# Last norm before the gate: transposing the plain stream and applying the row factor in the sigmoid

## The reference, cut to what matters

```python
def rmsnorm_2(x, w):
    xf = x.astype(jnp.float32)
    y = xf * lax.rsqrt(jnp.mean(xf * xf, axis=-1, keepdims=True) + EPS)
    return (y * w.astype(jnp.float32)).astype(x.dtype)

h = h + (jax.nn.silu(gate) * up) @ w_down[i]
ple_gate = jax.nn.sigmoid(rmsnorm_2(h, ple_norm_w[i]) @ w_ple_gate[i])
h = h + ple_gate * (p[i] @ w_ple_proj[i])
return rmsnorm_2(h, final_norm_w)
```

## Time and profile before

| | |
|---|---|
| median of the runs | 819.86 us (817.09 to 819.89) |
| span of the profiled execution | 815.9 us |
| PE busy | 780.6 us, 96% of the span |
| PEld / DVE / ACT / POOL busy | 669.7 / 540.0 / 414.7 / 92.5 us |
| granted PE clock, mean | 0.993 of full |

### The profile page before, as it was taken

One profiled execution on the slowest core, in us unless ns is written; L12 is line 12 of the kernel. 1 busy time (PEld: TensorE's weight loads), 2 busy tenths in 40 slices (PEclk: granted clock), 3 DMA queues, 4 the chain that ended last, 5 costly groups with the idle time before them and its releaser, 6 DMA issues. The chain is left out here.

```text
span 815.9 us, 11773 instructions
## 1 busy us (share of the span) xinstructions
PE 780.6 (96%) x4599; PEld 669.7 (82%) x4599; DVE 540.0 (66%) x714; ACT 414.7 (51%) x582; POOL 92.5 (11%) x150
## 2 busy tenths in 40 slices
PE   4899999999999999999989999999999999999996
PEld 3777787777789898988789998988888998988884
DVE  0673789977588778887478786654466666654465
ACT  2623413453676776644266555556364545543264
POOL 4000130401100000000060313210100000000000
PEclk9999999999999999999999999999999999999998
DMA  9963667732456556669536342321465655545611
GB/s 309 361 242 119 217 241 254 277 131 91 129 189 199 168 191 206 206 219 322 182 82 206 104 156 54 105 102 52 153 205 185 206 170 190 192 155 194 226 59 51
DMA packets 107900, 144.83 MB, mean 178 GB/s; under 512 B 6343, under 2 KB 70352, under 8 KB 107856
## 3 DMA queue, kind: packets, MB, share of 16 engines
q1 hardware_dynamic: 100512, 137.38, 50.7%
q10 hardware_dynamic: 7280, 6.83, 2.7%
q0 software_dynamic: 64, 0.01, 0.0%
HBM read 142.10 MB, written 2.10 MB: 177 GB/s over the span
## 5 line engine op out<-in xcount | busy, mean ns | idle before, releaser
L2074 PE MATMUL ps<-h_parts,w_hi 128*128 128x512 f32 x504 | 179.6, 396 | 0.0
L1276 DVE TENSOR_TENSOR w_lo<-raw,w_hi 128x2048 fp32r<-128x2048 f32 (+1 forms) x61 | 135.6, 2230 | 63.9 <-ACT w_hi L666 63.7
L666 ACT CAST w_hi<-raw 128x2048 fp32r<-128x2048 f32 (+1 forms) x61 | 112.9, 1852 | 78.2 <-PE ps L1950 56.6
L2073 PE MATMUL ps<-h_parts,w_lo 128*128 128x256 f32 x504 | 140.5, 279 | 0.0
L1284 DVE TENSOR_TENSOR w_lo<-raw,w_hi 128x2048 fp32r<-128x2048 f32 x44 | 100.7, 2289 | 16.2 <-ACT w_hi L674 15.7
L2074 PEld LDWEIGHTS ps<-h_parts,w_hi 128*128 128x128 f32 x504 | 94.6, 188 | 19.5
L2073 PEld LDWEIGHTS ps<-h_parts,w_lo 128*128 128x128 f32 x504 | 95.0, 188 | 3.3
L674 ACT CAST w_hi<-raw 128x2048 fp32r<-128x2048 f32 x44 | 84.0, 1908 | 0.0
L1948 PE MATMUL ps<-w_hi,act_hi 128*128 128x512 f32 x176 | 69.0, 392 | 0.0
L1950 PE MATMUL ps<-w_hi,act_lo 128*128 128x512 f32 x176 | 68.5, 389 | 0.0
L1949 PE MATMUL ps<-w_lo,act_hi 128*128 128x512 f32 x176 | 68.5, 389 | 0.0
(11 more groups left out here) (419 smaller groups left out, 1557.4 us busy)
## 6 DMA issues: line engine op xcount, KB each, us to landing
raw<-in_ffn_up_w SPq DMA_DIRECT2D x22, 1024.0 KB, 5.0
raw<-in_w_gate_up SPq DMA_DIRECT2D x22, 1024.0 KB, 5.0
raw<-in_ada_w SPq DMA_DIRECT2D x16, 1024.0 KB, 5.2
raw<-in_w_in SPq DMA_DIRECT2D x14, 1024.0 KB, 5.2
raw<-in_m_in_w SPq DMA_DIRECT2D x11, 1024.0 KB, 5.2
raw<-in_ffn_down_w SPq DMA_DIRECT2D x10, 1024.0 KB, 5.3
raw<-in_w_down SPq DMA_DIRECT2D x10, 1024.0 KB, 5.0
raw<-in_m_out_w SPq DMA_DIRECT2D x4, 1024.0 KB, 5.0
```

Of the source, the lines that this page charges most:

```text
L666: act.copy(part_view(w_hi, s), raw_view(split[s])).then_inc(hi_ready, 1)
L1276: dve.tensor_tensor(part_view(w_lo, s), raw_view(split[s]), part_view(w_hi, s).bitcast(F32), ALU.subtract).then_inc(lo_ready, 1)
L2073: pe.matmul(both[:, 0], lo[:, k, w], h_hi[:, k, :], start=False, stop=False)
L2074: ins = pe.matmul(both, hi[:, k, w], h_parts[:, :, k, :], start=False, stop=k == KD - 1)
```

## The change

Blocks of the plain stream are transposed with the identity (`flip`, the helper at L2114 that the kernel uses for its other transposes); `diagonal` is dropped for this norm, and its wait with it. `tile_turned` waits for the stream's halves instead (`x_upd`). The feature factor is still applied in `tile_hi` and `tile_lo`. The row factor becomes the `scale` operand of the sigmoid that reads the product out of PSUM, a column with one number per token; the sigmoid of tile t waits for that tile's factor. On ACT `tile_hi(0)` now stands ahead of the third sum of squares and of the cast of the second group.

```diff
             for t in range(TT):
                 norm_half("norm5", 12, t, t, 0)
+            tile_hi(0)
             norm_half("norm5", 12, 2, 0, 1)
             hi_until(at["ple_g"][0] + 2)
-            tile_hi(0)
             norm_half("norm5", 12, 3, 1, 1)
...
-                    bank_out(sig[:, i % 2, :], i, "sig_ready", ACT.Sigmoid)
+                    if n == 0:
+                        act.wait_ge(S("rstd"), base("rstd", "norm5") + t + 1)
+                    r_ = SS["norm5"] + t
+                    act.activation(sig[:, i % 2, :], ps[:, i, :], ACT.Sigmoid, scale=rstd[:, r_:r_ + 1]).then_inc(S("sig_ready"), 1)
...
             residual(1, 0)
-            diagonal("norm5", 0, base("rstd", "norm5") + 1)
             lo_until(at["ple_g"][0] + 2)
...
             tile_lo(0)
-            diagonal("norm5", 1, base("rstd", "norm5") + 2)
...
-                pe.wait_ge(S("diag"), base("diag", "norm5") + t + 1)
                 for k in range(KD):
-                    ins = pe.matmul(tile_bank(t, k), x[:, t, k * P:(k + 1) * P], diag[:, t, :], start=True, stop=True)
+                    if k % 4 == 0:
+                        pe.wait_ge(S("x_upd"), 12 + TT * (k // 4) + t + 1)
+                    ins = flip(tile_bank(t, k), x[:, t, k * P:(k + 1) * P])
                     if k % 4 == 3:
                         ins.then_inc(S("tr"), 1)
```

More of the change, by code:

```diff
@@ L160, in two_blocks @@
             "t0_done": (("mix_out", 1), ("down", 1), ("att_out", 1), ("down2", 1), ("ple_g", 1)),
-            "diag": (("norm1", 4), ("norm2", 2), ("norm3", 2), ("norm4", 2), ("norm5", 2)),
+            "diag": (("norm1", 4), ("norm2", 2), ("norm3", 2), ("norm4", 2)),
         }
```

## The result

The changed kernel takes 822.33 us against 819.12, ratio 1.0057 with a 95% interval of 1.0037 to 1.0077: about half a per cent slower. Between the medians lie 3.2 us, where 3.9 was forecast. Timed a second time, beside another set of runs of the kernel before, it is 821.75 against 817.55, ratio 1.0052 [1.0034, 1.0070], 4.2 us between the medians.

A forecast was written before the change was run, and what follows sets the result against it. PE was taken as the bound, with almost no gap from 780 to 808 us. Terms: 2.9 + 0.15 - 0.91 + 0.1 + 0.1 = 2.3, plus 1.6 for the clock, 3.9 on 819.86: 823.8 us, range 819.8 to 826.4.

The forecast's parts named there:

- Transposes and the wait ahead of them: PE, tile 0: no wait for the diagonal and eight transposes in 0.79 us, so the next matmul starts 1.54 earlier.
- The bound that had transposes as slow as matmuls: PE: with transposes as slow as the old matmuls, only 0.3 us gained on the first tile, nothing on the second.
- The cast and the list behind it: ACT's second-group cast starts 3.2 us later, behind `tile_hi(0)`; DVE's list passes it on whole, `tile_lo(0)` at about 788.7.
- The pause: PE stands still 4.4 us before tile 0's low-part matmuls, waiting for DVE; these start 2.9 late.
- The second tile: PE, tile 1: transposes give back 0.91 us, less 0.1 because `tile_hi(1)` starts a little later against PE.
- The clock: PE's granted clock falls to 0.50 in the pause, making the matmuls behind it slow; cost 1.6 us.
- the clock holds: Rival: same pause on PE but no slow matmuls, 2.3 us later in all, 822.2; chance 0.22.
- the slow clock lasts: Rival: PE's clock falls early in the pause and stays low through tile 1, 5.5 us later, 825.4; chance 0.13.
- The sigmoid's scale: Last sigmoid in the tail: its scale column costs between 0 and 0.1 us, taken as 0.1.
- no change: Measured outcome for the whole kernel within about 0.5% (4.1 us), taken as what a measurement can tell; chance 0.58.
- slower: Measured outcome for the whole kernel more than about 4.1 us slower; chance 0.39.
- The rival on the other side: ACT passes its new order in time, so PE has no pause: 2.35 us gained, 817.5; chance 0.07.

The follow-up runs named there:

- e1: The changed kernel with ACT's old order: third sum of squares and second group's cast ahead of `tile_hi(0)` again; 817.03 us against 817.68, ratio 0.9986.
- e2: The kernel before with only `tile_hi(0)` moved ahead of the second group's cast on ACT; 824.04 us against 817.68, ratio 1.0058.
- e5: e1 plus, on PE, both groups' high products of tile 0, then tile 1's transposes, ahead of the low products; 815.96 us against 817.68, ratio 0.9973.
- e4: e5 without the early transposes of tile 1, which stand behind tile 0's low products again; 815.71 us in one run, against 817.55.
- e3: The changed kernel with 18 extra matmuls, their result unused, filling PE's pause on tile 0; 820.92 us against 817.68, ratio 1.0029.
- e6: e5 with ordinary float32 matmuls against the identity in place of its transposes; 816.95 us against 817.55, ratio 0.9995.

## Why the prediction was right, point by point

- **Transposes and the wait ahead of them.** 1.54 earlier for the first tile was forecast; from the landmark to the six matmuls it is 1.03 (779.22 to 780.25) against 2.56: 1.53. The bound that had transposes as slow as matmuls did not come true.
- **The cast and the list behind it.** A cast 3.2 later was forecast; against the landmark it is 3.26. `tile_lo(0)` starts 8.50 behind the landmark (787.72 - 779.22) against 5.24 before (785.49 - 780.25): 3.26 again, passed on whole, as e1 and e2 then showed from both sides.
- **The pause.** 4.4 forecast, 4.40 in the row. The low parts start 8.89 behind the landmark and before 5.84 (786.09 - 780.25), so they are 3.05 late where 2.9 was told.
- **The second tile.** This term was mis-sized. 0.91 back with 0.1 for a wait was forecast, but from the transposes' start to the next matmul it is 1.15 (793.54 to 794.69) where the transposes need 0.79: 0.36 of wait for ACT's first block, so 0.55 came back against the 1.70 of before. e5, which has no such wait, is 0.39 shorter than e4, which has it.
- **The clock.** 1.6 forecast. The four low-part matmuls take 1.37 (788.11 to 789.48) against 0.94 before (786.09 to 787.03): 0.43, of which 0.15 is DVE's pace. The eight behind them take 3.15 (789.48 to 792.63) and not 1.85 as in e3 (792.44 to 794.29): 1.30. Together 0.28 + 1.30 = 1.6, and e3 gets 1.6 back. The size was right, the moment was not: the prediction had the clock fall in the pause, and it fell 0.8 us behind the pause's end. All of the slow stretch came under matmuls, as at 84 us, from which the 1.6 was taken; by the prediction's own reckoning a fall early in the pause would have cost less. That the row at 84 us was a good measure is in part luck, since the clock had been at 0.50 from 78 to 80 us too, ahead of the pause of 2.06. The rivals "the clock holds" and "the slow clock lasts" did not happen in the two profiles of this kernel.
- **The sigmoid's scale.** 0.69 in the tail against 0.60: 0.09, as bounded.
- **The sum.** On the profiled execution: stretch +4.25, tail +0.08 (819.2 - 810.90 against 815.9 - 807.68), and the landmark 1.03 earlier by what other stages did, which makes the 3.3 between the spans. By the mechanism the change costs 4.3, where 2.3 + 1.6 = 3.9 was told; the difference is the second tile's wait (0.26) and the low parts (0.15). The ratios, 0.57 and 0.52% of 819, are 4.7 and 4.3 us.
- **The time and the chances.** That 822.33 lies near the 823.8 told is in part luck. The base was the median of three runs, 819.86; the larger sets of the kernel before have 817.68 and 817.55, so the base was some 2 us high and the cost 0.4 low. A run's time is 1.7 to 1.9 us above its own span in every run on record, so the profile of 815.9 was of a run of about 817.7 and not of the median one. The ends of the range do not follow from what is said of them: the cases of 822.2 and 825.4 with half of 2.8 give 820.8 and 826.8, not 819.8 and 826.4; the measured time lies in both. And "no change" had 0.58 because 4.1 us was taken for the least that a measurement can tell: both intervals, some 0.2% to either side, lie clear of 1, so "slower", at 0.39, was given too little.
- **The rival on the other side** (ACT in time, 2.35 faster) needed the cast early; e1 gives it that, and the stretch is 0.55 shorter than before, not 2.35, since the low parts still bind by 0.76 and tile 1 waits. Only with PE's list rearranged, in e5, is it 1.88.

## What to carry to other kernels

Before an instruction is moved up on an engine that works down a list, look at what the engine waits for at the new place and at what then stands behind it: here 2 us of blocks and 0.8 us of a sum of squares went ahead of a cast that could have started 0.4 us before them (0.50 behind the landmark against 0.94), and the delay ran through a second engine's list to the bound engine. A pause on PE can have a second price behind it, in the clock; count the slow matmuls, and if a pause can't be avoided, other products that are ready may stand in it, as the second group's high products do in e5. To judge changes of a few microseconds, measure between two landmarks in the trace, since the medians carry the luck of the other stages.

## What the runs showed of the hardware that was not expected

The clock did not fall in the pauses of this place but behind them. It was at 1.00 through 4.40 us without a matmul (two profiles) and through 3.21 (e2), and fell each time 0.5 to 0.8 us after PE had begun again.

The same pause can be followed by a slow clock in one profile and not in another. Ahead of the transposes of an earlier norm PE waits about 2.36 us in every profile of this study; before, the window behind it had 1.00, in the changed kernel, whose program is the same there, it is

```profile
416.00:420.00 4.00, 4.00 (x24) 4.00 (x24) 2.74 (x7) 3.61 (x9) 3.45 (x9) 0.60 0.11 6
```

Four of the nine profiles have the fall there (both of the changed kernel, e5 and e6), five have not; what decides it stays open. From the end of that wait to the matmuls that start at 422.75 in both of these profiles it takes 6.21 us before (from 416.54) and 7.26 in the changed kernel (from 415.49). Such falls may be part of the 2 to 4 us by which runs of one kernel differ; no two profiles of one kernel differ in this one, so that is not shown.

Eight transposes with the identity and eight ordinary float32 matmuls of the same blocks differ by a factor of 2.15 on PE (0.79 us in e5, 1.70 in e6), not by the 4 that the prediction quotes. The sigmoid with a scale column takes 0.69 us where the one without took 0.60; the Trainium skill, "ScalarE: Activation LUTs", section "What ACT_TABLE_LOAD costs", puts a per-partition pointer operand at about 93 ns, and the trace agrees.
